# Backward products on the off-diagonal quarters of the matrix engine, and T turned by the matrix engine, in the chunked RWKV-7 part of a one-layer hybrid step

## The reference, cut to what matters

```python
def _wkv7_scan(r, w, k, v, kk, a, s0, reverse):
    def step(s, inp):
        r_t, w_t, k_t, v_t, kk_t, a_t = inp
        sa = jnp.einsum("bhvk,bhk->bhv", s, -kk_t)
        s = (s * w_t[:, :, None, :] + sa[..., None] * (kk_t * a_t)[:, :, None, :]
             + v_t[..., None] * k_t[:, :, None, :])
        return s, jnp.einsum("bhvk,bhk->bhv", s, r_t)
```

## Time and profile before

| | |
|---|---|
| median of 3 runs | 1368.11 us |
| profiled execution, its own time | 1369.97 us |
| its span, first to last instruction | 1368.2 us |
| mean granted PE clock | 0.983 of full |
| PE busy | 1289.2 us (94%), 13903 MATMUL records |
| PE weight loads busy | 1191.0 us (87%) |
| DVE busy | 689.7 us (50%) |
| ACT busy | 550.7 us (40%) |
| POOL busy | 42.2 us (3%) |

### The profile page before, as it was taken

One profiled execution on the slowest core, in us unless ns is written; L12 is line 12 of the kernel. 1 busy time (PEld: TensorE's weight loads), 2 busy tenths in 40 slices (PEclk: granted clock), 3 DMA queues, 4 the chain that ended last, 5 costly groups with the idle time before them and its releaser, 6 DMA issues.

```text
span 1368.2 us, 31729 instructions
## 1 busy us (share of the span) xinstructions
PE 1289.2 (94%) x13903; PEld 1191.0 (87%) x13903; DVE 689.7 (50%) x1036; ACT 550.7 (40%) x864; POOL 42.2 (3%) x103
## 2 busy tenths in 40 slices
PE   4899999998999779999999999899999999999995
PEld 1899999998999554489989878799999999999995
DVE  3427742642544666565547512554554544533544
ACT  3635534432233577624342212733433334333433
POOL 0100011000010000000000000000000000000000
PEclk9899999999999999999999999999999999999998
DMA  9422265315000200010116495022121121022222
GB/s 389 147 72 101 100 267 183 119 49 210 9 5 4 93 1 1 0 54 4 39 42 230 172 376 185 10 87 89 61 92 61 63 90 38 23 77 73 72 71 93
DMA packets 24027, 131.70 MB, mean 96 GB/s; under 512 B 2896, under 2 KB 3664, under 8 KB 15344
## 3 DMA queue, kind: packets, MB, share of 16 engines
q1 hardware_dynamic: 19104, 103.98, 21.7%
q0 software_dynamic: 4816, 26.11, 5.1%
HBM read 111.74 MB, written 18.34 MB: 95 GB/s over the span
## 4 chain that ended last, share of the span: by engine, by line
PE 58%; DVE 4%; ACT 3%; DMA 1%; issue 1%; DVEq 0%; ACTq 0%
PE ps L715 29%; PE ps L1230 11%; PE ps L885 2%; PE ps L873 2%; PE ps L1096 2%; PE ps L853 1%; PE ps L740 1%; PE ps L759 1%; DMA adl<-in_wada 1%; DVE nmax L1995 1%; PE ps L750 1%; PE ps L1002 1%; PE ps L1072 1%; PE ps L865 1%; PE ps L1043 1%
## 5 line engine op out<-in xcount | busy, mean ns | idle before, releaser
L715 PE MATMUL ps<-h2lo,whi 128*128 128x322 f32 x672 | 154.5, 311 | 0.7 <-ACT facc L1332 0.7
L715 PE MATMUL ps<-h2hi,wlo 128*128 128x322 f32 x672 | 155.0, 312 | 0.0
L715 PE MATMUL ps<-h2hi,whi 128*128 128x322 f32 x672 | 154.0, 310 | 0.0
L1685 DVE TENSOR_TENSOR wlo<-raw,whi 128x2048 fp32r<-128x2048 f32 x47 | 107.5, 2288 | 75.1 <-ACT whi L1293 75.1
L715 PE MATMUL ps<-hlo,whi 128*128 128x322 f32 x544 | 127.9, 316 | 1.0 <-ACT qkv L1358 1.0
L715 PE MATMUL ps<-hhi,wlo 128*128 128x322 f32 x544 | 125.4, 312 | 0.0
L715 PE MATMUL ps<-hhi,whi 128*128 128x322 f32 x544 | 124.7, 310 | 0.0
L715 PEld LDWEIGHTS ps<-h2hi,whi 128*128 128x128 f32 x672 | 114.2, 190 | 0.0
L715 PEld LDWEIGHTS ps<-h2lo,whi 128*128 128x128 f32 x672 | 113.0, 189 | 0.9 <-DVE wlo L1685 0.9
L715 PEld LDWEIGHTS ps<-h2hi,wlo 128*128 128x128 f32 x672 | 113.7, 189 | 0.0
L1732 DVE SCALAR_TENSOR_TENSOR facc<-fraw,par,facc 128x642 f32<-128x642 f32 x44 | 39.0, 887 | 137.3 <-ACT facc L1332 137.3
(11 more groups left out here) (353 smaller groups left out, 2592.7 us busy)
## 6 DMA issues: line engine op xcount, KB each, us to landing
raw<-in_wblk SPq DMA_DIRECT2D x48, 1024.0 KB, 4.9
adl<-in_wada SPq DMA_DIRECT2D x8, 2048.0 KB, 8.1
raw<-in_wdn SPq DMA_DIRECT2D x44, 256.0 KB, 2.6
adaw<-in_wada SPq DMA_DIRECT2D x4, 2048.0 KB, 20.3
gate_scratch<-gout POOLq DMA_DIRECT2D x16, 322.0 KB, 2.5
gld<-gate_scratch POOLq DMA_DIRECT2D x8, 644.0 KB, 4.6
attention_inputs_used<-attention_scratch SPq DMA_DIRECT2D x1, 5056.0 KB, 15.4
u_scratch<-uout POOLq DMA_DIRECT2D x12, 320.0 KB, 2.4
```

The costliest lines, as they stand in the source:

```text
L715: mm = pe.matmul(o, w, v, start=first, stop=last and w is hi and x is xh[n])
L1685: TT(wlo[s][:, :], raw[s][:, :], whi[s][:, :].bitcast(F32), ALU.subtract).then_inc(lo_done, 1)
```

## The change

For direction d = 1 the calls of H, P and the G and U stages take input rows of one half and write output rows of the other, the upper right and lower left quarters of the array; each direction gets a bank of its own (`b0 + d`, `b2 + d`). H issues a second set of products, T times the identity, into the columns beside H (`turn`), so that ACT's one copy to `hr` (512 columns in two banks) carries both H and the turned T; the turned T takes R's place in G, so DVE's V1 to V4 fall away and `rm` is written by ACT after H5 in a second copy. G5 stays on the diagonal quarters. KA and its mask AK move to the end of a round; P0, U0 and S0 move ahead of H1. `smid` and `tm` move in memory. P's calls are ordered so that the four quarters alternate. The waits are changed to match.

```diff
--- before.py
+++ after.py
@@ -299,6 +299,7 @@
     wcur = [w[:, 0:2 * P].rearrange("p (d n) -> p d n", d=2) for w in hpw]
     gcur = [w[:, 2 * P:3 * P] for w in hpw]
     stv = [w[:, 3 * P:4 * P].rearrange("p (d n) -> p d n", d=2) for w in hpw]
+    smid = [sb(f"smid{s}", [P, 2, CH]) for s in range(2)]
     assert spot[0] <= keep_u, (spot[0], keep_u)
     ESIZE = NC * (CH + 1)
 
@@ -322,16 +323,15 @@
             for s in range(2):
                 made[s].insert(0, sb(f"{name}{s}_{g}", [P, 2, 2, 2, CH]))
         if g:
-            tm = [sb(f"tm{s}", [P, 2, 2, CH]) for s in range(2)]
-            hm = [sb(f"hm{s}", [P, 2, 2, CH]) for s in range(2)]
+            hr = [sb(f"hr{s}", [P, 2, 2, 2, CH]) for s in range(2)]
             assert spot[0] == ring_half
     for s in range(2):
         rm[s] += [sb(f"rm{s}_{g}", [P, 2, 2, CH]) for g in range(2)]
+    tm = [sb(f"tm{s}", [P, 2, 2, CH]) for s in range(2)]
     vt64 = [sb(f"vt64_{s}", [P, NC, CH]) for s in range(2)]
     pw = [sb(f"pw{s}", [P, 2, CH]) for s in range(2)]
     uw = [sb(f"uw{s}", [P, 2, CH]) for s in range(2)]
     si = [[sb(f"si{s}_{n}", [P, 2, CH]) for n in range(2)] for s in range(2)]
-    smid = [sb(f"smid{s}", [P, 2, CH]) for s in range(2)]
     ysum = [sb(f"ysum{s}", [P, NT, P]) for s in range(2)]
     rwo = [sb(f"rwo{s}", [P, TP]) for s in range(2)]
     assert spot[0] <= qa_used_at, (spot[0], qa_used_at)
@@ -487,10 +487,10 @@
 
 
     LAGGED = ("P0", "U0", "S0", "Y0", "P1", "U1", "S1", "Y1")
-    PE_ST = ["KB", "KA", "P0", "H1", "U0", "G1", "S0", "Y0", "H2", "G2", "P1", "H3", "U1", "G3", "S1", "Y1", "H4", "G4",
-             "TR", "H5", "G5"]
-    DV_ST = ["AB", "R0", "T0", "AK", "C1", "V1", "S0", "C2", "V2", "C3", "V3", "S1", "Y1", "C4", "V4", "V5"]
-    AC_ST = ["P0", "H1", "U0", "H2", "P1", "H3", "U1", "Y1", "H4", "TR", "H5"]
+    PE_ST = ["KB", "P0", "U0", "S0", "H1", "Y0", "G1", "H2", "P1", "G2", "U1", "H3", "S1", "G3", "H4", "Y1", "G4", "H5", "TR",
+             "G5", "KA"]
+    DV_ST = ["AB", "R0", "T0", "S0", "C1", "C2", "S1", "C3", "Y1", "C4", "V5", "AK"]
+    AC_ST = ["P0", "U0", "H1", "H2", "P1", "U1", "H3", "H4", "Y1", "H5", "TR"]
     PO_ST = ["R0"]
     ADDED = (0, 3, 4)
 
@@ -840,13 +840,13 @@
 
             first = g == 0 and q == 0
             if name in ("KB", "KA"):
-                if g == 0:
+                if name == "KA":
+                    ac("H5")
+                elif g == 0:
                     pe.wait_ge(dv_prep, 10 * it + 10)
-                elif name == "KA":
+                else:
                     dv("V5", g - 1)
-                else:
-                    ac("H5", g - 1)
-                b, src = (b1, bt[s]) if name == "KB" else (b0, kt[s])
+                b, src = (b0, bt[s]) if name == "KB" else (b1, kt[s])
                 for d in range(2):
                     for q in range(2):
                         for r in half:
@@ -867,46 +867,60 @@
             elif name[0] == "H":
                 l = int(name[1])
                 dv("T0" if l == 1 else f"C{l - 1}")
-                for d in range(2):
+                for turn in range(2):
                     for q in range(2):
-                        for r in half:
-                            mm = pe.matmul(bank(b1, CH, CH * (2 * d + q))[r], abm[s][g % 2][r, d, q, 0, :], tm[s][r, d, q, :],
-                                           start=True, stop=True)
+                        for d in range(2):
+                            for r, away in zip(half, half[::-1]):
+                                left, right = (tm[s][r, d, q, :], ident[r, r]) if turn else \
+                                    (abm[s][g % 2][r, d, q, 0, :], tm[s][r, d, q, :])
+                                mm = pe.matmul(bank(b0 + d, CH, CH * (2 * turn + q))[away if d else r], left, right,
+                                               start=True, stop=True)
             elif name[0] == "G":
                 l = int(name[1])
                 ac(f"H{l}")
-                dv("AK" if l == 1 else f"V{l - 1}")
-                for d in range(2):
-                    for q in range(2):
-                        for r in half:
-                            left, right = rm[s][g % 2][r, d, q, :], hm[s][r, d, q, :]
+                for q in range(2):
+                    for d in range(2):
+                        for r, away in zip(half, half[::-1]):
+                            at = away if d else r
                             if l == 5:
-                                left, right = right, left
-                            mm = pe.matmul(bank(b0, CH, CH * (2 * d + q))[r], left, right, start=True, stop=True)
+                                mm = pe.matmul(bank(b0, CH, 4 * CH + CH * (2 * d + q))[at], hr[s][at, d, 0, q, :],
+                                               rm[s][g % 2][at, d, q, :], start=True, stop=True)
+                            else:
+                                mm = pe.matmul(bank(b0 + d, CH, 4 * CH + CH * q)[r], hr[s][at, d, 1, q, :],
+                                               hr[s][at, d, 0, q, :], start=True, stop=True)
             elif name[0] == "P":
                 if q == 0:
                     ac("TR")
+                    dv("AK")
+                    if g > 0:
+                        if g - 1 in ADDED:
+                            dv("Y1", g - 1)
+                        else:
+                            ac("Y1", g - 1)
                     if g == 1:
                         pe.wait_ge(sl_done, it + 1)
                     elif g > 1:
                         dv("S1", g - 1)
                 else:
                     dv("S0")
-                for d in range(2):
-                    for r in half:
-                        mm = pe.matmul(bank(b2, CH, CH * d)[r], akm[s][g % 2][r, d, q, 0, :], vt64[s][r, chunk_of(g, d, q), :],
-                                       start=True, stop=first)
-                    if not first:
-                        for r in half:
-                            mm = pe.matmul(bank(b2, CH, CH * d)[r], ar[s][r, d, chunk_of(g, d, q), 0, :], state(q)[r, d, :],
-                                           start=False, stop=True)
+                    if g == NG - 1:
+                        pe.wait_ge(pe_g[s], at_stage(PE_ST, it, g, "Y0"))
+                for n in range(1 if first else 2):
+                    for d in range(2):
+                        for r, away in zip(half, half[::-1]):
+                            left, right = (ar[s][r, d, chunk_of(g, d, q), 0, :], state(q)[r, d, :]) if n else \
+                                (akm[s][g % 2][r, d, q, 0, :], vt64[s][r, chunk_of(g, d, q), :])
+                            mm = pe.matmul(bank(b2 + d, CH, 6 * CH)[away if d else r], left, right, start=n == 0,
+                                           stop=first or n == 1)
             elif name[0] == "U":
                 ac(f"P{q}")
                 if q == 0:
                     dv("V5")
                 for d in range(2):
-                    for r in half:
-                        mm = pe.matmul(bank(b2, CH, P + CH * d)[r], rm[s][g % 2][r, d, q, :], pw[s][r, d, :], start=True, stop=True)
+                    for r, away in zip(half, half[::-1]):
+                        at = away if d else r
+                        mm = pe.matmul(bank(b2 + d, CH, 7 * CH)[r], rm[s][g % 2][at, d, q, :], pw[s][at, d, :], start=True,
+                                       stop=True)
             elif name[0] == "S":
                 ac(f"U{q}")
                 for d in range(2):
@@ -920,11 +934,6 @@
                         mm = pe.matmul(out[r], bkt[s][g % 2][r, d, q, 0, :], uw[s][r, d, :], start=False, stop=True)
             else:
                 ac(f"U{q}")
-                if q == 0 and g > 0:
-                    if g - 1 in ADDED:
-                        dv("Y1", g - 1)
-                    else:
-                        ac("Y1", g - 1)
                 for d in range(2):
                     c = chunk_of(g, d, q)
                     out = bank(b3, CH, P * place_of(g, d) + CH * (c % 2))
@@ -1485,10 +1494,16 @@
                 b0, b1, b2, b3 = range(4 * s, 4 * s + 4)
                 ac.wait_ge(pe_g[s], at_stage(PE_ST, it, g, name))
                 if name[0] == "H":
-                    ins = ac.activation(hm[s][:, :, :, :].rearrange("p d q n -> p (d q n)"), bank(b1, 4 * CH), ACT.Copy)
+                    if name == "H5":
+                        ac.activation(hr[s][:, :, 0, :, :].rearrange("p d q n -> p d (q n)"), ps[:, b0:b0 + 2, 0:2 * CH], ACT.Copy)
+                        ins = ac.activation(rm[s][g % 2][:, :, :, :].rearrange("p d q n -> p d (q n)"),
+                                            ps[:, b0:b0 + 2, 2 * CH:4 * CH], ACT.Copy)
+                    else:
+                        ins = ac.activation(hr[s][:, :, :, :, :].rearrange("p d m q n -> p d (m q n)"),
+                                            ps[:, b0:b0 + 2, 0:4 * CH], ACT.Copy)
                 elif name[0] in "PU":
```

(24 more changed lines are left out.)

## The result

The changed kernel takes 1411.11 us (median of 4 runs, 1408.79 to 1414.36), the kernel before 1368.29 us on the same chip: ratio 1.0305, 95% interval 1.0273 to 1.0338. It is 3% slower; the forecast was 1370.0 us with a range up to 1388, so it was wrong.

A forecast was written before the change was run, and what follows sets the result against it. PE, busy 94% of the span, was taken to set the time of both passes. Order and quarters -6.0, moved copies +2.6, supply in round 0 +3.0 and elsewhere +2.3 gave +1.9 us on 1368.11: 1370.0 us, range 1364.5 to 1388.

The forecast's parts named there:

- Elsewhere a block lasts 3.4 us of diagonal work: Instruction supply outside round 0 of pass 1: code just short from G1 to H3, 0.2 to 0.5 us a round, +2.3.
- the two dry points: Round 0 of pass 1: PE runs out of code at block ends, 253 records apart between the first two PE starts.
- bound of +5: Upper bound on the +2.3 us supply term outside round 0 of pass 1, taking 2.9 us instead of 2.5.
- twice the calls, on twice the quarters, in the same time: 0: H in a steady round: its doubled calls were priced at no added PE time.
- Four quarters at once: H, G, P, U: four 64x64 calls run in the time of two, 58 ns for four records.
- Rivals B and C: B: records no closer than 29 ns on average, 1424 us, chance 0.10. C: four take 62 to 72 ns, 1375-1389, 0.14.
- Blocks of 256 instructions: Instruction supply: PE reads its code in 16 KB blocks of 256 instructions and runs dry at a block's end.
- Round 0 of pass 1: Two issue gaps of 3 to 4 us, round 1 starting near 349; supply term +3.0 us, bounds 0 and +5.
- Steady rounds: From 23.8 us to 22.5 to 23.0 in pass 1 and 23.1 to 23.4 in pass 2.
- Waits of PE for DVE `tm`: Forecast sign: PE waits before H2, H4 and H5; chain less cover 0.47 us each for G1, G3 and G4.
- The order and the quarters, -6.0 us: Both passes: removed PE work less added waits gives -3.0 us a pass, -1.3 in rounds 2 and 3 each.
- Branch copies before pw in pass 2, +2.6: ACT's copies after H2 delay pw of P1 and U1, 0.5 to 0.9 us in each of rounds 1 to 3.

The follow-up runs named there:

- the run with the added work: Kernel before, with 480 unrolled calls on four quarters, 240 on two and a loop of 12 passes over 40 calls added after its last output: 1426.25 us.

## Why the prediction was wrong

The step that failed is the one under instruction supply that begins "Elsewhere a block lasts 3.4 us of diagonal work", with the term of +2.3 us at its end. The block, the two dry points and their place were right. The size was not: I set 2.5 us from packet to use against the time that a block lasts, and left out the 1.1 us between the entry into a block and the start of the next transfer. The whole cycle is 3.7 us, measured by the run with the added work. The 480 instructions from G1 to H3 are 1.9 blocks: at 2.5 us a block they take 4.7 us, just over the 4.4 of the stretch, but at 3.7 they take 6.9, which is 2.5 us over it and not 0.2 to 0.5. A steady round of the changed kernel has 902 records, 1804 instructions, 7.05 blocks: 7.05 x 3.7 = 26.1 us at least (26.7 measured), where the kernel before needs 5.8 x 3.7 = 21.4 and has 23.8. Against the 22.5 us that I forecast this is 3.6 us in each of eight rounds (1 to 4 of both passes), some 29 us where the sum has 2.3; "issue" in fact grew by 29 us. The prediction's bound of +5 held only the uncertainty of the number I had, not that of the quantity it stood for.

The length of a block in that step was off as well: a block is 256 instructions and not 235, so it lasts 3.7 us of diagonal work and not 3.4. That is the length of the cycle itself: work on two quarters stands at the limit, and the kernel before, at 4.1 us a block (23.8 over 5.8), near it.

With it fell the price of H: "twice the calls, on twice the quarters, in the same time: 0". The array does it in nearly the same time (0.98 us for 64 records with the restart, 0.93 forecast), but the code does not come in that time: 128 instructions at 3.7 us for 256 are 1.9 us.

Point by point:

- Four quarters at once: right, 58 ns for four records (61 with the restart), and G's 32 records, from 384.54, in about 0.5 us. Rivals B and C, which denied it, are out, since their condition (over 62 ns) was not met. The Trainium skill, TensorE: Matmul & The Clock Gate, "Wait — 56ns, not 53.3ns?", has a floor of about 25 ns from start to start; here records on four quarters start 14.5 ns apart on average, so for tiles that run side by side the trace disagrees. The prediction says that no row decides this; its own row of four column tiles, whose records start within 20 ns of each other, already stood against a floor between any two starts, though not against one for the average.
- Blocks of 256 instructions: right, to the instruction (128 + 128 from restart to restart). The Trainium skill, Advanced Engine Details and Errata, ISA Cache, gives two blocks of 256 instructions, and beside them 128 KB for TensorE; the trace agrees with the two blocks (some 386 instructions lay ready after 9.37 us of idle time) and not with the larger store. The loop of 160 instructions ran without a stop.
- Round 0 of pass 1: two stops of 3 to 4 us forecast, 2.6 and 2.5 us by the view of waits (some 2.8 from start to start); round 1 from 350.60 instead of near 349, from a start 2.1 us later. The round is 27.0 us long, 27.3 forecast, but the parts differ: the two gaps grew by 1.6 us together (only the first grew, from 0.8 to 2.6 us), and the same round in pass 2, where only 1.7 us of stops stand, grew by 4.3 us (17.0 to 21.3) instead of 1.7. So order and latency cost more than I had put down, the two gaps less, and that the length came out is partly luck.
- Steady rounds: 22.5 to 23.0 us forecast in pass 1, 26.7 measured.
- Waits of PE for DVE `tm`: present, 0.4 us each on average, 12 in pass 1. In all, 9 us of waits for results a pass stand where none stood.
- The order and the quarters, -6.0 us: not borne out. With DVE turning, so that the supply bites little (8.8 us of "issue" in both passes), the sum of order, copies and quarters is +7 us instead of a gain. The chain is longer there by the transposes, so this is no clean measure of the changed order; what it would do with PE turning and enough code was not tried.
- Branch copies before pw in pass 2, +2.6: not seen. PE's waits for pw are 1.0 us in pass 2 and 1.1 in pass 1; pass 2 lost 18.8 us, pass 1 19.7. That the dry stops left slack for them is likely, but no run tests it.

The chance of 0.54 for slower was on the right side, but for other reasons: 0.24 of it was for rivals that are refuted, and the other 0.30 for a time up to 1375 us.

## What to carry to other kernels

In unrolled code count instructions, not only array time: here 256 new instructions cost at least 3.7 us of PE, 29 ns for a MATMUL with its LDWEIGHTS, so a smaller tile of work on more quarters gains only until that rate. Before moving work from a half idle engine to the bound one as many small calls, compare the new count of instructions in a round times that rate with the round's length. A stop called "issue" in the middle of a stage, at equal distances in instructions, is the mark of it; large transfers beside it lengthen it (to 3.8 us here).

## What the runs showed of the hardware that was not expected

- The cycle of 3.74 us for 256 instructions holds with the DMA engines idle but for it: 1.12 us to the start of the transfer, 1.20 in it, 1.42 to the first instruction. Others were 3.4 to 4.0 us long.
- On two diagonal quarters the array needs 29 ns a record and the supply gives one in 29 ns; this balance hid the supply in the kernel before (whose only stops in the passes are the three of the earlier trace rows).
- Beside a bulk transfer a stop grew to 3.8 us (DMA share 0.84 in it), since the packet of code began over 5 us after the restart, and cutting the transfer up moved the cost and shortened it, but did not remove it.
- Changing the tile between 64*8 and 64*64 costs: a pair of calls 0.38 us at 2.4 GHz and 0.53 us at 1.2 GHz. The Trainium skill, TensorEngine Tiling (Array Packing), Key Properties, says that a change of mode drains the engine; the cost fits that, though no row shows the draining itself. With the lower clock that came with it (mean 0.88) the kernel was 28% slower.
- Records of 8 columns with loads of 64 stand 29 ns apart on two quarters, like those of 64 columns.
